# Hybrid encoder layer with product-key experts: gate tables as one 256-column split product a token, added by VectorE, with the one-hots on GpSimd

## What is computed

```python
q = (xc @ wq).reshape(PEER_CHUNK, PEER_HEADS, 2, PEER_HALF)
s = jnp.einsum('chpe,hpke->chpk', q, sk)              # 8 heads x 2 halves x 128 keys
sv, si = lax.top_k(s, PEER_TOPK)                      # 16 of each half
comb = sv[:, :, 0, :, None] + sv[:, :, 1, None, :]
cv, ci = lax.top_k(comb, PEER_TOPK)                   # 16 of the 256 pairs
e = i1 * PEER_NKEYS + i2
g = jax.nn.softmax(cv, axis=-1)
hid = jnp.einsum('cd,chkd->chk', xc, u[e])
out = jnp.einsum('chk,chkd->cd', gelu(hid) * g, v[e])
```

## Time and profile before

| | us |
|---|---|
| median of 3 runs | 1953.53 (1952.97 to 1955.05) |
| the profiled execution | 1954.08 |
| its span | 1952.2 |
| TensorE busy | 1930.9 (99%) |
| VectorE busy | 1644.9 (84%) |
| ScalarE busy | 976.8 (50%) |
| GpSimd busy | 825.9 (42%) |

### The profile page before, as it was taken

The page is one execution under the profiler, slowest core; times in us unless marked ns, Lnnn a source line. Parts: engine busy times, 40 slices in busy tenths (PEclk is TensorE's granted clock), DMA queues, the critical chain, the costliest instruction groups (busy, mean ns, idle before and its releaser), DMA issues.

```text
span 1952.2 us, 28726 instructions
## 1 busy us (share of the span) xinstructions
PE 1930.9 (99%) x10140; PEld 1655.2 (85%) x10140; DVE 1644.9 (84%) x3150; ACT 976.8 (50%) x2045; POOL 825.9 (42%) x590
## 2 busy tenths in 40 slices
PE   8999999999999999999999999999999999999999
PEld 8989989887888888888888888888888888888887
DVE  4887246879999999999977777799999999889898
ACT  4277153335788787788877762332222222222231
POOL 1345002010333333333456565555556656656563
PEclk9999999999999999999999999999999999999999
DMA  7100412235889988989899999999999999999996
GB/s 265 43 31 2 161 76 97 72 128 185 267 293 320 326 293 297 324 310 309 299 383 396 404 398 413 354 358 406 400 407 401 406 404 404 401 406 406 402 400 253
DMA packets 203365, 580.83 MB, mean 298 GB/s; under 512 B 19936, under 2 KB 57696, under 8 KB 201056
## 3 DMA queue, kind: packets, MB, share of 16 engines
q0 software_dynamic: 73728, 268.47, 36.9%
q1 hardware_dynamic: 60192, 179.69, 24.8%
q10 hardware_dynamic: 69312, 130.97, 17.8%
HBM read 504.60 MB, written 74.45 MB: 297 GB/s over the span
## 4 chain that ended last, share of the span: by engine, by line
PE 80%; DVE 8%; DMA 7%; ACT 2%; issue 2%; POOL 1%; SPq 0%; ACTq 0%; DVEq 0%
PE ps L337 24%; PE ps L338 24%; PE ps L339 24%; PE ps L1532 5%; DMA ring_c<-in_v,expert_ids 1%; DMA ring_b<-in_v,expert_ids 1%; DMA gel_dram<-arena_b 1%; PE ps L1493 1%; DMA arena_a<-in_x_prompt 1%; DMA ring_a<-in_v,expert_ids 1%; PE ps L1406 1%; DVE sparse L1207 1%; DVE arena_b L1091 1%; DMA ring_a<-in_u_rows,expert_ids 0%; DVE arena_b L1088 0%
## 5 line engine op out<-in xcount | busy, mean ns | idle before, releaser
L337 PE MATMUL ps<-v_hi_slots,w_lo 128*128 128x512 f32 x1024 | 398.8, 389 | 0.3 <-DVE w_lo L1237 0.3
L339 PE MATMUL ps<-v_hi_slots,w_lo 128*128 128x512 f32 x1024 | 398.4, 389 | 0.0
L337 PE MATMUL ps<-feat_hi,w_hi 128*128 128x512 f32 (+1 forms) x936 | 360.2, 385 | 1.2 <-DVE w_lo L1109 0.7
L338 PE MATMUL ps<-feat_lo,w_hi 128*128 128x512 f32 (+1 forms) x936 | 351.2, 375 | 0.0
L339 PE MATMUL ps<-feat_hi,w_lo 128*128 128x512 f32 (+1 forms) x936 | 351.0, 375 | 0.0
L732 ACT ACTIVATE w_lo<-arena_a 128x512 fp32r<-128x512 f32 x128 | 81.0, 633 | 488.2 <-DVE arena_a L1231 253.8
L847 POOL DMA_INDIRECT ring_a<-in_u_rows,expert_ids x86 | 120.6, 1403 | 322.4 <-DVE ring_a L1199 187.5
L337 PEld LDWEIGHTS ps<-v_hi_slots,w_lo 128*128 128x128 f32 x1024 | 192.2, 188 | 41.7 <-DVE w_lo L1237 2.0
L339 PEld LDWEIGHTS ps<-v_hi_slots,w_lo 128*128 128x128 f32 x1024 | 192.2, 188 | 40.0
L339 PEld LDWEIGHTS ps<-feat_hi,w_lo 128*128 128x128 f32 x936 | 176.1, 188 | 31.8
L337 PEld LDWEIGHTS ps<-feat_hi,w_hi 128*128 128x128 f32 x936 | 176.6, 189 | 30.4 <-DVE w_lo L1109 1.4
(11 more groups left out here) (224 smaller groups left out, 4462.6 us busy)
## 6 DMA issues: line engine op xcount, KB each, us to landing
arena_a<-in_v ACTq DMA_DIRECT2D x121, 512.0 KB, 7.8
w_raw<-in_uT SPq DMA_DIRECT2D x85, 512.0 KB, 6.6
g_dram<-arena_a ACTq DMA_DIRECT2D x64, 512.0 KB, 7.6
gel_dram<-arena_b ACTq DMA_DIRECT2D x120, 256.0 KB, 5.4
w_raw<-gel_dram SPq DMA_DIRECT2D x120, 256.0 KB, 8.1
arena_a<-in_uT SPq DMA_DIRECT2D x43, 512.0 KB
w_raw<-in_w_all SPq DMA_DIRECT2D x16, 1024.0 KB, 6.0
arena_b<-g_dram SPq DMA_DIRECT2D x32, 512.0 KB, 11.3
```

What stands on the lines that cost most here:

```text
L337: nc.tensor.matmul(out, lh, rh, start=first, stop=False)
L338: nc.tensor.matmul(out, lh, rl, start=False, stop=False)
L339: return nc.tensor.matmul(out, ll, rh, start=False, stop=last)
```

## The change

The one-hots and gates become float32r. The one-hot of i1 is exact in it; the gate is cut into a high part (`gate_hi`) and a rest, and for each token `gated` holds two blocks of 128 columns: one-hot times high part, one-hot times rest. `gate_table` is one float32r matmul of 256 columns a token, whose two halves are the table of high parts and the table of rests, in PSUM side by side; a group takes two banks, so two groups in flight take banks 3 to 6, the expert products keep three banks (e % 3) instead of four, and `flip_params` moves to bank 7. ScalarE copies the high tables to SBUF (`g_hi`), and a new VectorE operation, `gates_sum`, adds the rests from PSUM and signals `g_ev`. Both one-hots move to GpSimd: 8 operations `tensor_scalar` of 128 columns a group, in a loop that interleaves them with the gathers. ScalarE's two passes become a scaling by the high part and one by the rest. `dots_by` is made flatter up to slab 113 and steeper behind it, `store_g` comes a slab later. Core of the diff (blank lines and hunk headers left out):

```diff
--- before.py
+++ after.py
...
 def dots_by(e):
-    return min(5 * max(min(e - 6, 75), 0) // 3 + 11 * max(e - 81, 0) // 4, 243)
+    return min(3 * max(min(e - 6, 75), 0) // 2 + 13 * max(min(e - 81, 32), 0) // 5 + 16 * max(e - 113, 0) // 5, 243)
 def items_by(e):
...
         ua_hi, ua_lo = at("ua_hi", 24576 + 13312, 1024, F32R), at("ua_lo", 24576 + 14336, 1024, F32R)
         vh_ = at("v_hi_slots", 24576 + 4096, 4096, F32R)
         vla_, vlb_ = at("v_lo_slots_a", 24576 + 8192, 2048, F32R), at("v_lo_slots_b", 24576 + 15360, 2048, F32R)
+        oh_ = at("one_hots", 12288, 2048, F32R)
+        ga_, gb_ = at("gated_a", 24576 + 15360, 2048, F32R), at("gated_b", 20480, 2048, F32R)
+        ghi_ = at("gate_hi", 24576 + 17408, 256, F32R)
         Gb_ = at("gates_b", 0, 4096)
         yf_ = at("y_final", 6144, 4096)
         ps = ctx.enter_context(nc.psum_tensor("ps", [P, 8, 512], F32))
...
         ur = [view(w, a, KD, P) for w, a in ((A_, 12288), (Wr_, 2048), (Wr_, 3072))]
         uh = [view(w, a, KD, P) for w, a in ((ua_hi, 0), (Wh_, 2048), (Wh_, 3072))]
         ul = [view(w, a, KD, P) for w, a in ((ua_lo, 0), (Wl_, 2048), (Wl_, 3072))]
-        oh_2 = view(Wr_, 0, 4, SG, P)
-        oh_g = view(A_, 15360, 4, SG, P)
+        oh_2 = view(oh_, 0, 4, SG, P)
+        gated = [view(w, 1024 * i, SG, 2, P) for w in (ga_, gb_) for i in range(2)]
+        gate_hi = view(ghi_, 0, 2, P)
         Gst = view(A_, 0, 2, NK, BLK)
         s_in = view(A_, 9216, 2, 2, P)
         gel = view(B_, 0, 3, NDEN)
...
         CE = view(B_, 2752, HEADS, TOPK)
         par = view(B_, 4864, 2, 3, P)
         eq = view(B_, 3648, 4, TOPK, TOPK)
-        G_ps = [ps[:, b, :].rearrange("p (t i) -> p i t", i=P) for b in (4, 5)]
+        G_ps = [ps[:, b:b + 2, :].rearrange("p b x -> p (b x)").rearrange("p (t h i) -> p h i t", h=2, i=P)
+                for b in (3, 5)]
         si_u = [view(b, 0, 4, 2, TOPK) for b in (iu, iu2)]
         ci_u = [b[:, 128:192] for b in (iu, iu2)]
         ab_u = view(iu2, 192, 2, 64)
...
         u_hi, u_lo, h_mm, gelu_ok = (sem(n) for n in ("u_hi", "u_lo", "h_mm", "gelu_ok"))
         gel_out = [sem(f"gel_out{i}") for i in range(3)]
         s_load = [sem(f"s_load{i}") for i in range(2)]
-        s_read, oh2_ok, oh1_ok, ohg_ok, g_mm, g_ev = (
-            sem(n) for n in ("s_read", "oh2_ok", "oh1_ok", "ohg_ok", "g_mm", "g_ev"))
+        s_read, oh2_ok, oh1_ok, ohg_ok, g_mm, g_hi, g_ev = (
+            sem(n) for n in ("s_read", "oh2_ok", "oh1_ok", "ohg_ok", "g_mm", "g_hi", "g_ev"))
         g_out = [sem(f"g_out{i}") for i in range(2)]
         ce_ok, ce_exp, gate_ok, gts_ok, par_tr, par_ev = (
             sem(n) for n in ("ce_ok", "ce_exp", "gate_ok", "gts_ok", "par_tr", "par_ev"))
...
                 score_out(7, i)
             def gated_one_hots(g):
-                t = g // 32
-                act.wait_ge(par_ev, t + 1)
-                if g >= 4:
-                    act.wait_ge(g_mm, g - 3)
-                c = (g % 32) * SG
+                t, c = g // 32, (g % 32) * SG
+                act.wait_ge(oh1_ok, g + 1)
                 for n in range(SG):
-                    nc.scalar.activation(oh_g[:, g % 4, n, :], iota[:, :], ACT.Abs, scale=-1.0,
-                                         bias=par[:, t % 2, 0, c + n:c + n + 1]).then_inc(oh1_ok, 1)
-                act.wait_ge(oh1_ok, SG * g + SG)
+                    nc.scalar.activation(gated[g % 4][:, n, 0, :], gated[g % 4][:, n, 1, :].bitcast(F32), ACT.Copy,
+                                         scale=gate_hi[:, t % 2, c + n:c + n + 1].bitcast(F32))
                 for n in range(SG):
-                    ins = nc.scalar.activation(oh_g[:, g % 4, n, :], oh_g[:, g % 4, n, :], ACT.Relu, scale=-4.0,
-                                               bias=par[:, t % 2, 2, c + n:c + n + 1])
+                    ins = nc.scalar.activation(gated[g % 4][:, n, 1, :], gated[g % 4][:, n, 1, :].bitcast(F32),
+                                               ACT.Copy, scale=par[:, t % 2, 2, c + n:c + n + 1])
                 ins.then_inc(ohg_ok, 1)
             def gates_out(g):
...
                 act.wait_ge(g_mm, g + 1)
                 if g % 8 == 0 and b >= 2:
                     act.wait_ge(g_out[b % 2], 64 * (b // 2))
-                nc.scalar.activation(Gst[:, b % 2, :, (g % 8) * SG:(g % 8 + 1) * SG], G_ps[g % 2],
-                                     ACT.Copy).then_inc(g_ev, 1)
+                nc.scalar.activation(Gst[:, b % 2, :, (g % 8) * SG:(g % 8 + 1) * SG], G_ps[g % 2][:, 0, :, :],
+                                     ACT.Copy).then_inc(g_hi, 1)
             def exp_of(t):
                 act.wait_ge(ce_ok, softmax_tiles.index(t) + 1)
...
                     act.wait_ge(g_mm, NG_DEN)
                 elif NK - 4 <= e < NK - 1:
                     act.wait_ge(gel_out[e % 3], 16 * (NK - CH) // 3)
-                nc.scalar.activation(gel[:, e % 3, :] if e < NK - CH else gel_kept[e - NK + CH], ps[:, e % 4, :],
+                nc.scalar.activation(gel[:, e % 3, :] if e < NK - CH else gel_kept[e - NK + CH], ps[:, e % 3, :],
                                      ACT.Gelu).then_inc(gelu_ok, 1)
                 if e + 3 < NK:
                     u_split_hi(e + 3)
...
                     act.wait_ge(gelu_ok, e + 1)
                     act.dma_start(gel_dram[e], gel[:, e % 3, :]).then_inc(gel_out[e % 3], 16)
                 for b in range(NBLK):
-                    if 0 <= e - group_slab(8 * b + 7) - 1 < 4:
-                        store_g(b, e - group_slab(8 * b + 7) - 1)
+                    if 0 <= e - group_slab(8 * b + 7) - 2 < 4:
+                        store_g(b, e - group_slab(8 * b + 7) - 2)
                 for g in groups_in(e):
                     gates_out(g)
                 for g in groups_in(e + 2):
...
                     out=ring[n % RING], out_offset=None, in_=io["u_rows"] if n < DOTS else v_rows,
                     in_offset=bass.IndirectOffsetOnAxis(ap=eidx[:, s, j:j + 1], axis=0)).then_inc(row_in[n % RING], 16)
+            def one_hots(g):
+                t, c = g // 32, (g % 32) * SG
+                pool.wait_ge(par_ev, t + 1)
+                if g >= 4:
+                    pool.wait_ge(g_mm, g - 3)
+                for dst, p, ok in ((oh_2[:, g % 4, :, :], 1, oh2_ok), (gated[g % 4][:, :, 1, :], 0, oh1_ok)):
+                    for n in range(SG):
+                        ins = nc.gpsimd.tensor_scalar(dst[:, n, :], iota[:, :], par[:, t % 2, p, c + n:c + n + 1],
+                                                      None, ALU.is_equal)
+                    ins.then_inc(ok, 1)
+
             pool.wait_ge(qp_mm, 4 * HEADS)
-            before_v = dots_by(NK - 1)
-            for n in range(before_v + 2):
-                gather(n)
-            sent = before_v + 2
+            before_v, sent = dots_by(NK - 1), 0
+            for e in range(NK):
+                for g in groups_in(e + 3):
+                    one_hots(g)
+                while sent < min(dots_by(e) + RING, before_v + 2):
+                    gather(sent)
+                    sent += 1
             for e in range(NK):
                 while sent < min(ITEMS, items_by(e) + 3):
                     gather(sent)
...
                 tt(e, e, srec8.unsqueeze(2).to_broadcast([P, HEADS, TOPK]), ALU.mult
                    ).then_inc(gts_ok if t >= DT else gate_ok, 1)
-            def one_hots(g):
-                t = g // 32
-                dve.wait_ge(par_ev, t + 1)
-                if g >= 4:
-                    dve.wait_ge(g_mm, g - 3)
-                c = (g % 32) * SG
-                tt(oh_2[:, g % 4, :, :], iota[:, :].unsqueeze(1).to_broadcast([P, SG, P]),
-                   par[:, t % 2, 1, c:c + SG].unsqueeze(2).to_broadcast([P, SG, P]), ALU.is_equal
-                   ).then_inc(oh2_ok, 1)
+            def gates_sum(g):
+                b = g // 8
+                rows = Gst[:, b % 2, :, (g % 8) * SG:(g % 8 + 1) * SG]
+                dve.wait_ge(g_hi, g + 1)
+                tt(rows, G_ps[g % 2][:, 1, :, :], rows, ALU.add).then_inc(g_ev, 1)
             def take_params(t):
                 dve.wait_ge(par_tr, t + 1)
                 if t >= 2:
                     dve.wait_ge(ohg_ok, 32 * (t - 1))
-                nc.vector.tensor_copy(par[:, t % 2, :, :],
-                                      ps[:, 6, 0:384].rearrange("p (a b) -> p a b", a=3)).then_inc(par_ev, 1)
+                steps.did(nc.vector.tensor_copy(par[:, t % 2, 0:2, :],
+                                                ps[:, 7, 0:256].rearrange("p (a b) -> p a b", a=2)))
+                steps.step(nc.vector.tensor_copy(gate_hi[:, t % 2, :], ps[:, 7, 256:384]))
+                tt(par[:, t % 2, 2, :], ps[:, 7, 256:384], gate_hi[:, t % 2, :].bitcast(F32), ALU.subtract
+                   ).then_inc(par_ev, 1)
             def part(q):
                 quad, r = q // 15, q % 15
...
             for e in range(NK):
                 if 3 <= e < NK - 3:
                     u_split_lo(e + 3)
```

(18 more changed lines are left out.)

## The result

The changed kernel takes 2372.12 us (median of 4, 2370.79 to 2374.63) against 1953.62 before: ratio 1.2148, 95% interval 1.2133 to 1.2163. The forecast was 2028 with a range of 1932 to 2120. The profiled execution has a span of 2369.9 us, 417.7 more than before. The direction was right, the size far off.

What follows compares the result with a forecast made beforehand. TensorE was taken to bound the kernel before, GpSimd and VectorE to set the pace after: +34 (slabs 8 to 80), +32 (81 to 112) and +8 (113 to 127) on 1954.1 us gave 2028 us, range 1932 to 2120.

Steps and rivals of the forecast that it cites:

- TensorE's product: Gate tables on TensorE: a group costs 0.48 us instead of 0.90, 54 us less over 128 groups.
- The wait at the table: TensorE at the gate table waits 0.9 us for VectorE's sum, 46 times, 41 us, if VectorE is punctual.
- all 46 slabs: The two slabs behind each of 23 slabs with two groups, where TensorE was to wait for VectorE's sum.
- GpSimd's price: A 128-column one-hot on GpSimd takes 0.35 us, range 0.25 to 0.50; 3.4 us a slab.
- The estimate of 0.30 us from the Trainium skill: GpSimd one-hot at 1.03 cycles an element for one input: 0.30 us, and a kernel time near 1990 us.
- The lock: GpSimd and VectorE exclude each other at SBUF; VectorE charged 0.15 us per two-input operation, 0.6 us a slab.
- the pace: Time per slab set by GpSimd and VectorE: 7.05 us in slabs 8 to 80, 7.6 in 81 to 112.
- GpSimd outright: Rival: GpSimd alone bounds slabs 8 to 112, 2210 us at 0.50 us a one-hot; chance 0.18 (above 2085).
- Punctual engines: Rival: one-hots cost 0.25 us or less, lock rarely met, TensorE's loop decides: -13, 1941 us; chance 0.22.
- Clean gain: Rival: sums arrive before TensorE wants them, no wait at the table: -54, 1900 us; chance 0.06.
- Slabs 113 to 127 and the second loop: More gathers (44 instead of 30) under full DMA: +8 us, between 0 and 18; second loop 0.
- ScalarE and three banks: ScalarE's work unchanged and covered, 0; three PSUM banks instead of four cost 0 unless ScalarE is two slabs late.

Runs made afterwards that it cites:

- e2: Changed kernel with GpSimd's 8 one-hot operations a group cut to 2 of one column from the fifth group on: 2022.0 us, ratio 1.0354.
- e11: As e2, with VectorE's sum of the rests left out too and ScalarE's copy giving the signal: 1947.7 us, ratio 0.9970.
- e1: Separate kernel without the layer, only GpSimd operations alone and beside VectorE's: a one-hot of 128 columns takes 0.58 us alone.
- e9: Changed kernel with VectorE's dots reading 16 columns instead of 1024: 2212.6 us, ratio 1.1325.
- e7: Kernel before the change with the new dots_by schedule and nothing else: 1970.8 us, ratio 1.0099.
- e5: As e2, with the slab's first gate table behind step 5 instead of step 3: 1987.3 us, ratio 1.0172.
- e6: As e5, with dots_by as in the kernel before the change: 1971.7 us, ratio 1.0105.

## Why the prediction was wrong in size

**TensorE's product, right in price, not in what it brings.** 0.47 us a group in e2 where 0.48 was worked out from the earlier trace rows. e11 shows half of the 54 us as time, 27 us, all in slabs 8 to 80; in slabs 81 to 112, with DMA at 0.98, none.

**The wait at the table, right in place and in its single size, short in sum.** The mechanism of the earlier trace rows is what e2 shows, 0.87 us where VectorE is punctual. "Each lateness adds" was written and then charged at nothing: 67 us by e2 against e11 (VectorE's 85 us of work for the sum gone with it), not 41. The term was taken as if VectorE started its split on time in all 46 slabs, with a load of 6.2 us in a slab of 6.4. The strided read of PSUM cost nothing (0.680 against the 0.69 taken).

**GpSimd's price, the step that failed.** 0.35 us with a bound of 0.50, measured 0.58 alone and 0.82 in the kernel. The slope came from a `tensor_tensor` and a memset, on the thought that one stream lies between none and two. It does not: 2.5 ns a column against the 1.67 of two streams. "An operation that the trace does not show lies between its neighbours" was the assumption, and the bound built on it was none. The estimate of 0.30 us from the Trainium skill, "GPSIMD Engine Reference", section "Performance versus the Vector engine" (1.03 cycles an element, which the page gives for at most two operations an element, read there as one input), is contradicted by e1's 0.58.

**The lock, right as a mechanism, charged to the wrong engine.** VectorE was to lose 0.15 us an operation and lost 0.03 (1.246 against 1.219) as long as GpSimd's operations were short; GpSimd lost 0.24 a one-hot (0.82 - 0.58), 1024 times, 246 us. The earlier trace rows showed both directions. Per slab it was 9.8 x 0.24 = 2.4 us, where the pace had 1.2 to 1.8 for "about one to two long waits" in slabs 8 to 80 and at most 1 in the others. Counted by VectorE's long operations, 105 splits, 191 dots and 32 of the decode in the stage, it is 0.75 us for each; e9 gives 0.73 for a dot.

**The sum again with measured terms**: 9.8 one-hots at 0.82 are 8.0 us, 1.8 gathers a slab at 1.12 and 0.23 of issue are 2.4, together 10.4 us; the 1089 us are 10.4 a slab. That is bookkeeping, since the 0.82 is read in the same trace, but it says that the form of the forecast, GpSimd's load per slab, was the right one, and that the one-hots, taken at 3.4 us with 1 to 2 of waits, were what was too low; the gathers were not. The part of the 353 us of the one-hots that is the lock can't be had from one run. Worked out it is the 246 us above; e9 shows 154 us of stage for the dots' share of it.

**The rivals.** GpSimd outright, at 0.18, was what happened, beyond its own 2210: 9.7 and 11.8 us a slab against its 8.5 and 10.3. Its upper price should have set the range. *Punctual engines* had a rule for its end, about 0.27 us a one-hot, and e2 puts this at nearly zero cost and still finds 1.0354, so -13 would not have been had at any price: the late sums and the dots were missing in it. *Clean gain* needed the sum out of the way; e11 gives that and gets 0.3%. Its other way, the sum ahead of the split in VectorE's order, wasn't tried.

**Slips in the sums.** At 0.42 us a one-hot slabs 81 to 112 are 4.1 + 4.4 + 1 = 9.5 us and not 9.0, so that case is 2127 and not 2113. A pace of 6.8 to 8.2 us over 105 slabs with the 8 behind gives 1984 to 2131, not 1965 to 2085. And 0.05 us less a one-hot is 51 us, so the estimate from the Trainium skill would come to a time near 1977, not 1990. None of them would have reached 2372.

**Slabs 113 to 127 and the second loop.** +8 forecast with 18 as the upper bound, +24.8 measured. The dots' schedule is 17 us of it in the kernel before (e7) and 21.6 in the changed one (e5 less e6), so the upper bound of 18, 14 rows at the rate of a full DMA, was about the size and not the limit. The place was another: slabs 113 to 127 took 82 us as against 79, and most of the rest is VectorE's late splits at the start of the loop that was called untouched. From 1647 to 1700 TensorE is idle 11 us, with a granted clock of 0.90. The cause that was forecast, rows that come late, fits e9, where the loss stays with dots of 16 columns.

**ScalarE and three banks.** No change as work (its copy out of PSUM has a median of 0.592 us for a group; three banks 1.0001). But ScalarE waits 519 us, and it is it that carries GpSimd's lateness on to VectorE.

**What stays open.** What the lower clock adds. TensorE is busy 773.4 us in the stage; before it was 689.9, and with 54 less to issue it would be 636, so 137 us more are mostly matmuls at the lower level. GpSimd was idle only 46 of 1089 us, so little of that can be on the path; this is argued and no run separates it. And e1 shows what each engine's operation costs the other, 0.09 us for a one-hot and 1.78 for two products of 1024 columns, not why GpSimd's share is so small.

## What to carry over

Price an operation that the trace has never shown by a run of it alone, or leave the bound open upwards: "between two others that I know" isn't a bound. When two engines exclude one another, measure in a small kernel what each costs the other, and count the long operations of the one: here each of VectorE's 1.2 us cost GpSimd about 0.75. And when a signal moves to an engine that runs at over 90% of the slab, count its lateness and not its duration: the 0.68 us sum cost 67 us in all and ate the whole gain of the product. And before counting on less work of one engine, look at what else is full in each stretch: where DMA was at 1.01, 16 us less issued brought nothing.

## What was not expected of the hardware

- On GpSimd the one-input `tensor_scalar` of 128 columns (0.58 us, 0.50 with a constant) is dearer than the two-input `tensor_tensor` with a broadcast operand (0.36); at 512 columns 1.54 against 1.00.
- Beside back-to-back two-input operations of VectorE of 1024 columns (1.14 us apart) GpSimd gets one one-hot through for every two of them, in 2.36 us, and costs VectorE 0.09 with it. With two-input operations of 1.0 us in the kernel GpSimd gets them at 1.1, and VectorE's splits go from 1.22 to 1.90.
- TensorE's matmuls of 512 columns go from a pitch of 0.23 to 0.43 us after idling for 6 us, and back within the slab.
